# Two load lines of the spectrum stage change places in the sync engine's queue

## The reference, cut to what matters

```python
def _bidir_long_conv(u, k_freq, bias):
    L = u.shape[1]
    u_freq = jnp.fft.rfft(u, n=2 * L, axis=1)
    y = jnp.fft.irfft(u_freq * k_freq[None], n=2 * L, axis=1)[:, :L]
    return y + u * bias.astype(jnp.float32)

z = v
for o, g in enumerate((x1, x2)):
    z = g * _bidir_long_conv(z, k_freq[:, o], bias[o])
```

## Time and profile before

| | |
|---|---|
| median of 3 runs | 1241.09 us |
| lowest, highest | 1240.59, 1245.46 us |
| the profiled execution's own time | 1241.09 us |
| its span in the trace | 1239.3 us |
| busy over the span: PE, DVE, ACT | 1107.0, 850.9, 569.1 us |

### The profile page before, as it was taken

How to read it: one execution, slowest core, us unless ns; L and a number is a source line. 1 busy time by engine, 2 the same in 40 slices (tenths; PEclk the granted TensorE clock), 3 DMA queues, 4 the chain that set the end, 5 groups by cost and what they waited for, 6 DMA issues and landing times. The chain is left out here.

```text
span 1239.3 us, 14298 instructions
## 1 busy us (share of the span) xinstructions
PE 1107.0 (89%) x4928; PEld 852.1 (69%) x4928; DVE 850.9 (69%) x1093; ACT 569.1 (46%) x745; POOL 12.5 (1%) x32
## 2 busy tenths in 40 slices
PE   3899589999999999889999988898898748999996
PEld 0277368888888777667888765676676527888884
DVE  6599784555454638359999445646989666787877
ACT  4078643444545345337777434334786633222210
POOL 0001000000000000000000000000000000000000
PEclk8799889999999999999999988999989968999998
DMA  9869953677675445778998578758898597375521
GB/s 350 284 199 310 326 206 120 211 238 245 222 247 170 146 142 188 245 197 254 276 279 244 176 205 259 237 192 240 267 295 249 190 347 226 132 220 163 171 88 64
DMA packets 154990, 273.25 MB, mean 220 GB/s; under 512 B 11488, under 2 KB 49504, under 8 KB 153253
## 3 DMA queue, kind: packets, MB, share of 16 engines
q1 hardware_dynamic: 151461, 266.74, 67.0%
q0 software_dynamic: 3168, 5.51, 1.9%
q10 hardware_dynamic: 288, 0.08, 0.0%
HBM read 178.95 MB, written 98.57 MB: 224 GB/s over the span
## 5 line engine op out<-in xcount | busy, mean ns | idle before, releaser
L176 PE MATMUL u_pp<-u_uhi,prj_whi 128*128 128x512 f32 x768 | 312.6, 407 | 21.5 <-DMA p_first<-in_t_kfirst 10.6
L177 PE MATMUL u_pp<-u_ulo,prj_whi 128*128 128x512 f32 x768 | 307.7, 401 | 0.0
L178 PE MATMUL u_pp<-u_uhi,prj_wlo 128*128 128x512 f32 x768 | 306.9, 400 | 0.0
L176 PEld LDWEIGHTS u_pp<-u_uhi,prj_whi 128*128 128x128 f32 x768 | 148.2, 193 | 64.5 <-issue 20.4
L178 PEld LDWEIGHTS u_pp<-u_uhi,prj_wlo 128*128 128x128 f32 x768 | 147.7, 192 | 35.1
L177 PEld LDWEIGHTS u_pp<-u_ulo,prj_whi 128*128 128x128 f32 x768 | 148.2, 193 | 33.2
L1241 DVE TENSOR_TENSOR p_alo<-p_a,p_ahi 128x1024 fp32r<-128x1024 f32 x32 | 39.2, 1225 | 101.0 <-ACT p_ahi L1182 101.0
L176 PE MATMUL end_ps<-end_whl,prj_whi 128*128 128x512 f32 x256 | 101.2, 395 | 2.4 <-DVE prj_wlo L2136 2.4
L178 PE MATMUL end_ps<-end_whl,prj_wlo 128*128 128x512 f32 x256 | 101.1, 395 | 0.0
L177 PE MATMUL end_ps<-end_whl,prj_whi 128*128 128x512 f32 x256 | 101.0, 395 | 0.0
L1182 ACT ACTIVATE p_ahi<-p_a 128x1024 fp32r<-128x1024 f32 x32 | 34.0, 1061 | 126.3 <-PE p_ps L178 121.7
(11 more groups left out here) (195 smaller groups left out, 1969.5 us busy)
## 6 DMA issues: line engine op xcount, KB each, us to landing
p_a<-kseq SPq DMA_DIRECT2D x32, 512.0 KB, 4.3
kfreq<-p_out SPq DMA_DIRECT2D x32, 512.0 KB, 5.2
xseq<-p_xo SPq DMA_DIRECT2D x32, 512.0 KB, 7.6
p_k_re<-kfreq SPq DMA_DIRECT2D x64, 256.0 KB, 6.1
p_k_im<-kfreq SPq DMA_DIRECT2D x64, 256.0 KB, 4.3
bseq<-p_out SPq DMA_DIRECT2D x32, 512.0 KB, 4.8
prj_ws<-in_t_win SPq DMA_DIRECT2D x24, 512.0 KB
kseq<-prj_row SPq DMA_DIRECT2D x22, 512.0 KB
```

Of the source, the lines that this page charges most:

```text
L176: nc.tensor.matmul(out, w[0], m[0], start=start, stop=False, skip_group_check=True)
L177: nc.tensor.matmul(out, w[0], m[1], start=False, stop=False, skip_group_check=True)
L178: return nc.tensor.matmul(out, w[1], m[0], start=False, stop=stop, skip_group_check=True)
```

## The change

In each step of `spectrum_product` SP issues the load of k_re ahead of the load of a. Nothing else is touched, and the loads before the loop stay as they were.

```diff
             for step in range(plan.lo, S):
                 if 0 <= step < NU:
+                    load_k_re(step + 2)
                     load_a(step + 2)
-                    load_k_re(step + 2)
                     load_k_im(step + 1)
```

## The result

Median 1257.96 us (1254.26 to 1258.74, 4 runs) against 1241.86 us (1240.59 to 1245.46, 4 runs); ratio 1.0115, 95% interval 1.0088 to 1.0142. Some 16 us were lost where I had forecast none. The profiled execution after took 1257.63 us. Of 21 executions of it two ran in a slower state, at a granted clock of 0.74 and 0.56 (1413.84 and 1829.60 us), and are left out; the others lie between 1250.49 and 1262.23 us.

The account below looks back on a forecast made before the run. TensorE was taken to bound p3, and the chain from straight to ylow partly p5. 0 (p3) + 0.9 (p5, crowded) - 1.0 (two starts) = -0.1 us gave 1241.0 us, likeliest put at 1241.5; range 1237 to 1248.

Parts of the forecast that it names:

- What is moved: SP's queue, p3 and p5: only a(s + 2) issues later, some 3 to 8 us; no store or load behind it moves.
- The rooms: 28 steps of p3 and p5: a has 4.9 to 6.9 us from issue before ahigh would delay the swap behind it.
- How long a takes: Load of a behind k_re: 4.4 us uncrowded, costing nothing; crowded, 0.3 us later than the old landing, bound 1.3 us.
- the term of 0.9 us: p5: three crowded steps without room beyond the old landing take 0.3 us each, +0.9 us together, +3.6 at the bound.
- The bound: Crowded steps: at most 1.3 us for a, k_re's 512 KB at about 400 GB/s, if a waits for all of k_re.
- Ring order: DMA engines: by the skill's rule a waits for all of k_re, 1.3 us, sum about 2.7 us higher; landings suggested otherwise.
- Where it is paid: Late swaps: nothing in p3, +0.9 us in three crowded steps of p5, 0 if hidden in VectorE's order.
- p3: 0: p3: a late swap costs 0, as the inverse product began 1.9 us after its low half of y was done.
- What comes back: Start of each stage: a of unit 2 leaves the queued transfers, -0.5 us per stage, between 0 and -2.3 us.
- B: Rival, mostly p5: a becomes late, landing at 6.4 us, some 13 us lost; 1254, or 1247.5 passed on by half; chance 0.14.
- C: Rival, both starts and p5: earlier k_im, a(1) and stores remove TensorE's waits, faster, 1232.6 us; chance 0.06.
- D: Rival: the change does nothing, a waiting at the DMA engines and not at SP; 1241 us, inside the no-change case's 0.80.

Follow-up runs that it names:

- experiment 1: Against the kernel before: order a, then k_re kept, but SP waits for straight(s) in front of both; 1245.49 us, ratio 1.0024.
- Experiments 1 and 2: Against the kernel before, all behind the wait for straight: a ahead of k_re, 1245.49 us; a between k_re's two halves, 1252.75 us, ratio 1.0072.

## Why the prediction was wrong, point by point

- **What is moved: right but for the late steps.** The same instructions; a behind the wait, 1.27 us behind k_re's issue; in most steps k_im and the stores not moved. But where a was late, `turned` was late too, and k_im, which waits for it, went out 4.5 to 5.5 us behind k_re (at 591.60, 631.84, 669.83 and 913.55) where it had been 2.6 to 3.6 us in every step before. The issue of a didn't hold it up; the lateness of a came round to it.
- **The rooms: right.** a was to reach ScalarE within 4.9 to 6.9 us of its issue, and issue by itself is not what costs: with a first behind the same wait, 3 or 4 us in all (experiment 1).
- **How long a takes: the step that failed.** I took 4.4 us uncrowded and a delay of 0.3 us, bound 1.3, for its place against k_re when crowded. Measured: 5.3 to 6.1 us uncrowded in p3, 5.3 to 6.4 in p5, 7.5 to 9.1 crowded. So the term of 0.9 us (0.3 us in three steps) was far too small: in the crowded step above alone a landed 3.4 us later, and p5 paid some 6 us. Two errors are in it. The bound took k_re at a's 400 GB/s; it moves at about 225, so its 512 KB are 2.3 us. And that an old a and an old k_re had landed together was read as "the place is worth 0.3 us". In that step a had been issued 2.7 us ahead of k_re. After the change the a of the same step was issued at 592.87, 3.8 us later than before, and again took 9.1 us: the whole delay of its issue reached its landing. A common landing says that the backlog is common, not that the later one could be issued later still.
- **Ring order.** The Trainium skill, "DMA: Bandwidth & Descriptors", section "Queues, rings and completion order", has the engines take descriptors in ring order, which the prediction weighed and set aside. Experiments 1 and 2 agree with its direction: a's wait grows with what is ahead of it. Taking it up would not have saved the forecast: with the 2.7 us that it was to add, the sum is 1243.7 us. The size here comes from the strip's 225 GB/s.
- **Where it is paid: wrong for p3, the second step that failed.** The term "p3: 0" measured 0.74%, some 8 or 9 us. The slack of 1.9 us in front of one inverse product was read as p3's slack. VectorE is busy for 127.39 of 136 us there, and behind the late `turned` and `add` stand the convolution and the transposes that wait for it: 7.5 us of TensorE's time for 1.7 before. With the waits for the low half of y (2.5 for 0.4) and for `alow` (1.6 for 2.3) that is 7.2 of the 7.5 us by which its idle time grew in p3. p5 paid 0.45%.
- **What comes back: about nothing.** In the first step of p3 `ahigh(1)` waited 7.1 us for 7.9, TensorE 1.6 for 2.3: 0.7 us, near the 0.5 that I took. In p5 `ahigh(1)` waited 6.9 us for 6.7, so nothing came back. The stores of `bseq` were to land a little earlier and landed later, 6.0 us for 4.8 in the median, and k_im 5.3 for 4.3.
- **The rivals.** B was right in kind and in its condition: a at 5.7 us and above in most steps, the rooms of p5 failing one by one, ScalarE waiting in nearly all of p5's. Its total was near by luck. It gave some 13 us to p5 and little to p3; p5 paid 6 us, about what B gave when passed on by half (1247.5 us; p5 alone measured 1247.97), and p3 paid the rest. Its slowest load was also too quick, 6.4 us, where a took up to 9.1. It had 0.14. It was set aside by "4.3 us was enough", a row of a load with no other load ahead of it. C and D did not happen.

## What to carry to other kernels

When two loads in one queue change places, price each by the rate at which *its own* bytes move beside the other's, read from the DMA strip with the order of issue beside it; here two loads of 512 KB differ by 1.8 (about 400 and 225 GB/s). Where the DMA engines are near full, rank all transfers of a step by how soon each is waited for: moving one ahead, or even fetching it a unit earlier, can make the ones behind it late. And a slack read in front of one matmul is not that of its stage: look at what else stands in the queue of the engine that becomes late.

## What the runs showed of the hardware

- Loads that fill 64 partitions at a time (k_re, k_im, 2 x 256 KB) moved at about 225 GB/s, one of 512 KB over all 128 at about 400 GB/s. Both move in packets of about 2 KB (314 packets for 0.61 MB in the fast stretch of experiment 1, 473 for 0.85 MB in the slow one), so the packet size is not the difference. That the half of the partitions is the cause was not tested by itself; they also read every second row, and the same rows twice.
- A transfer issued later can land earlier: the a issued at 583.97 landed at 592.9, the first half of k_im, issued at 585.72, at 592.6.
- How long a load takes goes with what is queued around it: the a issued at 583.97 took 8.9 us, with two `vx` stores, a `bseq` store and a weight load issued at 578.08 to 580.68 ahead of k_re, and more stores behind; that of 566.09, with neither `vx` stores nor a weight load near, 5.5 us. What the transfers behind it add was not measured apart from those ahead.
